# Low-weight ring 32 bytes further along, and the activation buffers placed anew against both weight rings, in a one-core hybrid decoder layer

## The chip, the core and the metric

The kernel is one program on one core of a Trainium2 chip. The metric is device time in microseconds (us) of that core; 1393.51 us is the median of three runs before the change (1393.4 to 1394.25). All arithmetic is in fp32. TensorE multiplies in its fp32r form (a faster, rounded kind of fp32), and each large product is split in a high and a low part so that the result keeps fp32 accuracy.

## What is computed

One layer of a decoder, 256 tokens wide, model width 2048. Cut to what matters:

```
h      = rms_norm(x, norm_mix_g);  proj = h @ w_in                 # 2048 -> 8*512 + 3*2048
o_a, o_b, o_c = hgrn2(...), s5(...), stick_breaking(...)           # three mixers, width 512 each
merged = sum_k sigmoid(gate_k) * (o_k @ w_branch[k]);  x = x + merged @ w_out
up     = causal_depthwise_conv(rms_norm(x, norm_ffn_g) @ w_up, conv_w)   # 2048 -> 2*5632
x      = x + (silu(up[..., :D_FF]) * up[..., D_FF:]) @ w_down            # 5632 -> 2048
```

## The kernel before

Weights stream from HBM in pieces of 8 blocks (a block is 128 x 128, 512 bytes a partition; a piece is 4096 bytes a partition) into a ring of four buffers `raw0` to `raw3`. ScalarE writes the high part of a piece to `w_hi` (L743), VectorE the difference to `w_lo` (L1076); both are rings of four too. Activations are kept transposed, features on the partitions and 256 tokens along the free dimension, with the high part and the low part of a feature tile side by side: `a_raw` and `a_in` (normed input, later the merged branches), `h2` (normed input of the up projection), `act` (hidden activations), and `o_hg`, `o_sb`, `o_s5`, `glu_in` for the branches. One k tile of these takes 2048 bytes a partition, 1024 of them high and 1024 low.

The stages follow one another on TensorE: input projection (tiles 0 to 63, mixers between tiles), GLU, three branches, output projection, up projection, down projection. SP's queue issues the weight loads in that order, each as soon as `w_lo` of the piece four before it is ready. A block is multiplied in one of two ways.

A **pair** (`piece`, L376 and L378), used for input tiles 0 to 7, GLU, output, up and down:

```
pe.matmul(bank[b][:, :], w[:, k * P:(k + 1) * P], a.rearrange("p a t -> p (a t)"), ...)      # w_hi x (high, low): 512 columns
mm = pe.matmul(bank[b][:, 0:SEQ], l[:, k * P:(k + 1) * P], a[:, 0, :], ...)                  # w_lo x high: 256 columns
```

A **triple** (`in_piece` L390, `branch_piece` L416, `plain_piece` L401), used for input tiles 8 to 63, the branches and the last output tile of down: three multiplies of 256 columns, `w_hi` x high, `w_hi` x low, `w_lo` x high. Either way 768 columns pass for one block, and each multiply has a weight load of its own.

TensorE holds one set of weights while the next is being loaded. In the trace a load starts within 0.01 us of the multiply ahead of the one it serves. So while the array streams one operand out of SBUF (the *moving* operand: an activation), the load reads another (the *stationary* operand: a weight block). In a pair, the `w_lo` block is loaded beside the 512-column multiply and the next `w_hi` block beside the 256-column one. In a triple, `w_hi` is loaded beside the first and the third multiply and `w_lo` beside the second.

Buffers have fixed addresses. Each tensor starts where the one before it ends, rounded up to 32 bytes; the names `late`, `early`, `mixing`, `within` and `splits` are scopes that lay several sets over the same space. A tensor called `apart` of 160 bytes a partition, which nothing uses, stands before the scopes:

```
rstd = sb("rstd", [P, SEQ])
var = sb("var", [P, SEQ])
root = sb("root", [P, SEQ])
sb("apart", [P, 40])

late = ExitStack()
act = sb("act", [P, FT, 2, SEQ], F32R, late)
x1 = sb("x1", [P, KT, SEQ], F32, late)
h2 = sb("h2", [P, KT, 2, SEQ], F32R, late)
```

A block is 512 bytes and a k tile 2048, so the distance of an activation buffer from a weight buffer, taken modulo 128, is the same for all blocks of a stage.

Of the kernel before, what the change touches and what calls it, by code (L numbers as in the profile page):

```python
# [38 lines left out]
F32 = mybir.dt.float32  # L39
# [6 lines left out]
P = 128  # L46
# [88 lines left out]
def layer(nc, xT, w_in, w_glu, w_br, w_out, w_up, w_down, norm_mix, norm_ffn, hg_gain, s5_small, s5_b, s5_c,  # L135
          s5_skip, sb_gain, conv, out):
    ctx = ExitStack()
    with ctx:
        def sb(name, shape, dt=F32, scope=None):
            return (scope or ctx).enter_context(nc.sbuf_tensor(name, shape, dt))  # L140


        raw = [sb(f"raw{s}", [P, PIECE * P]) for s in range(RING)]
        w_hi = [sb(f"w_hi{s}", [P, PIECE * P], F32R) for s in range(RING)]
        w_lo = [sb(f"w_lo{s}", [P, PIECE * P], F32R) for s in range(RING)]
        half = [sb(f"half{s}", [P, SEQ]) for s in range(2)]
        ones = sb("ones", [P, P], F32R)
# [18 lines left out]


        late = ExitStack()
        act = sb("act", [P, FT, 2, SEQ], F32R, late)
        x1 = sb("x1", [P, KT, SEQ], F32, late)  # L170
        h2 = sb("h2", [P, KT, 2, SEQ], F32R, late)
        sum_u = sb("sum_u", [P, 2, SEQ], F32, late)
        padded = sb("padded", [P, 2, SEQ + 2], F32, late)
# [3 lines left out]


        early = ExitStack()
        a_in = sb("a_in", [P, KT, 2, SEQ], F32R, early)  # L180
        head = ExitStack()
        x_first = sb("x_first", [P, KT, SEQ], F32, head)
# [1635 lines left out]
```

## Time and profile before

| | |
|---|---|
| median of 3 runs | 1393.51 us (1393.4 to 1394.25) |
| the profiled execution | 1393.05 us |
| its span on the core, first to last instruction | 1391.5 us |
| TensorE matmul busy | 1387.0 us (100%) |
| TensorE weight loads busy (beside matmuls) | 1280.6 us (92%) |
| VectorE busy | 1034.2 us (74%) |
| ScalarE busy | 755.1 us (54%) |
| GpSimd busy | 143.2 us (10%) |
| DMA queue of the weights | 255.89 MB, 57.8% of the 16 engines |

Busy time is the union of instruction records. Matmuls overlap in the pipeline, so a busy TensorE says only that something is in it; how fast it goes is read from the distance between the starts of two multiplies. 1.55 us of the profiled time lies around the span.

### The profile page before, as it was taken

What the parts mean: (1) busy time and instruction counts of PE and PEld (TensorE: products, weight loads), DVE (VectorE), ACT (ScalarE), POOL (GpSimd) and SP (SyncE); (2) the same over time, 40 slices, a digit from 0 to 9 for tenths busy, and PEclk for the clock granted to TensorE, in tenths of its full rate; (3) what the DMA queues carried; (4) which work ended last, traced back from release to release, by engine and by line L of the source; (5) the groups of instructions that cost most, each with busy time, mean ns of one, the idle gap of its engine ahead of it and who ended that gap; (6) DMA issues with size and microseconds to landing.
All of it is one profiled execution on the core that took longest, in us unless ns stands there. A gap on an engine that the chain in (4) does not pass through costs nothing.

```text
span 1391.5 us, 27921 instructions
## 1 busy us (share of the span) xinstructions
PE 1387.0 (100%) x9886; PEld 1280.6 (92%) x9886; DVE 1034.2 (74%) x1427; ACT 755.1 (54%) x1056; POOL 143.2 (10%) x187
## 2 busy tenths in 40 slices
PE   9999999999999999999999999999999999999999
PEld 8999999999999999988888888888888888888888
DVE  7999857899889678776687777777777775455453
ACT  7575676754544554545655555555555554444432
POOL 1200000000000024322111111111111110000000
PEclk9999999999999999999999999999999999999999
DMA  8655545446564656766566555655656656666663
GB/s 287 187 185 180 181 156 179 145 162 198 171 195 161 196 182 218 222 188 193 174 202 193 192 187 182 193 194 185 188 189 194 182 178 198 207 188 201 195 202 111
DMA packets 76513, 261.70 MB, mean 188 GB/s; under 512 B 8800, under 2 KB 10368, under 8 KB 76448
## 3 DMA queue, kind: packets, MB, share of 16 engines
q1 hardware_dynamic: 74304, 255.89, 57.8%
q0 software_dynamic: 1424, 4.37, 1.1%
q8 instruction: 46, 0.75, 0.2%
q10 hardware_dynamic: 720, 0.53, 0.1%
q14 instruction: 19, 0.16, 0.0%
HBM read 258.66 MB, written 2.10 MB: 187 GB/s over the span
## 4 chain that ended last, share of the span: by engine, by line
PE 98%; ACT 1%; DMA 1%; DVE 0%; SPq 0%; issue 0%; ACTq 0%
PE bank L376 40%; PE bank L390 28%; PE bank L378 21%; PE bank L416 5%; PE pair L435 1%; PE bank L401 1%; DMA x_first<-xT 0%; DMA raw<-w_in 0%; PE pair L572 0%; ACT w_hi L743 0%; ACT gates L753 0%; PE pair L441 0%; SPq L298 0%; PE pair L543 0%; ACT L753 0%
## 5 line engine op out<-in xcount | busy, mean ns | idle before, releaser
L1076 DVE TENSOR_TENSOR w_lo<-raw,w_hi 128x1024 fp32r<-128x1024 f32 x496 | 584.8, 1189 | 292.9 <-ACT w_hi L743 288.2
L743 ACT ACTIVATE w_hi<-raw 128x1024 fp32r<-128x1024 f32 x496 | 508.7, 1030 | 411.4 <-PE bank L378 198.5
L376 PE MATMUL bank<-h,w_hi 128*128 128x512 f32 x1408 | 488.4, 390 | 0.0
L378 PE MATMUL bank<-h,w_lo 128*128 128x256 f32 x1408 | 397.1, 282 | 0.0
L390 PE MATMUL bank<-a_in,w_hi 128*128 128x256 f32 x2048 | 362.1, 280 | 0.0
L376 PEld LDWEIGHTS bank<-h,w_hi 128*128 128x128 f32 x1408 | 264.4, 188 | 55.4
L390 PEld LDWEIGHTS bank<-a_in,w_hi 128*128 128x128 f32 x2048 | 311.8, 188 | 3.1 <-issue 2.1
L390 PE MATMUL bank<-a_in,w_lo 128*128 128x256 f32 x1024 | 285.6, 279 | 0.0
L378 PEld LDWEIGHTS bank<-h,w_lo 128*128 128x128 f32 x1408 | 266.1, 189 | 0.0
L376 PE MATMUL bank<-act,w_hi 128*128 128x512 f32 x660 | 228.8, 390 | 0.0
L390 PEld LDWEIGHTS bank<-a_in,w_lo 128*128 128x128 f32 x1024 | 192.5, 188 | 0.0
L378 PE MATMUL bank<-act,w_lo 128*128 128x256 f32 x660 | 186.1, 282 | 0.0
L376 PEld LDWEIGHTS bank<-act,w_hi 128*128 128x128 f32 x660 | 123.9, 188 | 26.0
L378 PEld LDWEIGHTS bank<-act,w_lo 128*128 128x128 f32 x660 | 124.7, 189 | 0.0
L1742 POOL TENSOR_TENSOR padded<-sum_u,rstd 128x256 f32<-128x256 f32 x88 | 73.9, 841 | 413.1 <-DVE sum_u L1097 400.3
L376 PE MATMUL bank<-a_in,w_hi 128*128 128x512 f32 x256 | 88.8, 390 | 0.0
L378 PE MATMUL bank<-a_in,w_lo 128*128 128x256 f32 x256 | 72.2, 282 | 0.0
L1016 ACT ACTIVATE silu<-convd 128x256 f32<-128x256 f32 x43 | 18.0, 418 | 95.9 <-DVE convd L1602 95.9
L1600 DVE SCALAR_TENSOR_TENSOR convd<-padded,taps,convd 128x256 f32<-128x256 f32 x88 | 62.7, 713 | 1.0 <-ACT convd L1036 1.0
L1602 DVE SCALAR_TENSOR_TENSOR convd<-padded,taps,convd 128x256 f32<-128x256 f32 x88 | 54.0, 614 | 11.5
L376 PEld LDWEIGHTS bank<-a_in,w_hi 128*128 128x128 f32 x256 | 48.1, 188 | 10.0
L750 ACT ACTIVATE half<-bank 128x256 f32<-128x256 f32 x135 | 49.4, 366 | 3.7 <-PE bank L378 3.6
(234 smaller groups left out, 1364.4 us busy)
## 6 DMA issues: line engine op xcount, KB each, us to landing
raw<-w_up SPq DMA_DIRECT2D x176, 512.0 KB, 3.7
raw<-w_in SPq DMA_DIRECT2D x156, 512.0 KB, 4.3
raw<-w_down SPq DMA_DIRECT2D x80, 512.0 KB, 4.4
raw<-w_out SPq DMA_DIRECT2D x32, 512.0 KB, 4.2
raw<-w_br SPq DMA_DIRECT2D x16, 512.0 KB, 3.6
raw<-w_br SPq DMA_DIRECT2D x16, 256.0 KB, 3.3
raw<-w_down SPq DMA_DIRECT2D x16, 256.0 KB, 2.7
x_first<-xT SPq DMA_DIRECT2D x8, 256.0 KB, 5.7
```

Of the source, the lines that this page charges most:

```text
L376: pe.matmul(bank[b][:, :], w[:, k * P:(k + 1) * P], a.rearrange("p a t -> p (a t)"), start=first and n == 0, stop=False, skip_group_check= ...
L378: mm = pe.matmul(bank[b][:, 0:SEQ], l[:, k * P:(k + 1) * P], a[:, 0, :], start=False, stop=last and n == len(blocks) - 1, skip_group_check ...
L390: mm = pe.matmul(bank[n % BANKS][:, 0:SEQ], x[:, k * P:(k + 1) * P], src[:, PIECE * h + k, part, :], start=h == 0 and k == 0 and m == 0, s ...
L401: mm = pe.matmul(bank[b][:, 0:SEQ], x[:, k * P:(k + 1) * P], rhs(k, part), start=first and k == 0 and m == 0, stop=last and k == blocks - ...
L416: mm = pe.matmul(bank[b][:, 0:SEQ], x[:, cols], src[:, k, part, :], start=k == 0 and m == 0, stop=k == CT - 1 and m == 2, skip_group_check ...
L743: act_e.activation(w_hi[s][:, 0:blocks * P], raw[s][:, 0:blocks * P], ACT.Copy).then_inc(hi_ready, 1)
L750: act_e.activation(half[j % 2][:, :], bank[j % BANKS][:, SEQ:2 * SEQ], ACT.Copy).then_inc(half_copied, 1)
L1016: act_e.activation(silu[:, :], convd[:, (j - 3) % 4, :], ACT.Silu).then_inc(S("silu_done"), 1)
L1076: ve.tensor_tensor(w_lo[s][:, w], raw[s][:, w], w_hi[s][:, w].bitcast(F32), ALU.subtract).then_inc(lo_ready, 1)
L1600: ve.scalar_tensor_tensor(c, padded[:, j % 2, 1:SEQ + 1], taps[:, t, 1:2], c, ALU.mult, ALU.add).then_inc(S("tap1"), 1)
L1602: ve.scalar_tensor_tensor(c, padded[:, j % 2, 0:SEQ], taps[:, t, 0:1], c, ALU.mult, ALU.add).then_inc(S("conv_done"), 1)
L1742: pool.tensor_tensor(padded[:, j, 2:], sum_u[:, j, :], rstd[:, :], ALU.mult).then_inc(S("up_scaled"), 1)
```

## The change

Four tensors that nothing reads or writes are added; no instruction is added, removed or moved, and every size and shape stays.

```
 raw = [sb(f"raw{s}", [P, PIECE * P]) for s in range(RING)]
 w_hi = [sb(f"w_hi{s}", [P, PIECE * P], F32R) for s in range(RING)]
+sb("apart_weights", [P, 8])
 w_lo = [sb(f"w_lo{s}", [P, PIECE * P], F32R) for s in range(RING)]
...
 late = ExitStack()
+sb("apart_act", [P, 8], F32, late)
 act = sb("act", [P, FT, 2, SEQ], F32R, late)
 x1 = sb("x1", [P, KT, SEQ], F32, late)
+sb("apart_h2", [P, 56], F32, late)
 h2 = sb("h2", [P, KT, 2, SEQ], F32R, late)
...
 early = ExitStack()
+sb("apart_in", [P, 56], F32, early)
 a_in = sb("a_in", [P, KT, 2, SEQ], F32R, early)
```

Start addresses a partition, modulo 128 bytes, as the declared sizes give them. The distances are those of the moving operand past `w_hi` and past `w_lo`, modulo 128 (modulo 256 they are the same numbers):

| buffer | before | after | past `w_hi`, before / after | past `w_lo`, before / after |
|---|---|---|---|---|
| `raw`, `w_hi` | 0 | 0 | | |
| `w_lo` | 0 | 32 | | |
| `a_raw`, `a_in`, `o_*`, `glu_in` | 32 | 32 | 32 / 32 | 32 / 0 |
| `h2` (up) | 32 | 64 | 32 / 64 | 32 / 32 |
| `act` (down) | 32 | 96 | 32 / 96 | 32 / 64 |
| `ones` | 0 | 32 | | |
| `eye`, `lower` | 32 | 64 | | |
| `x1` | 32 | 96 | | |
| `sum_u`, `padded` | 32 | 64 | | |
| `convd`, `silu` | 64 | 96 | | |
| mixers' `proj`, `tmp`, `softp`, `gates` | 32 | 32 | | |

## Rows read from the trace of the kernel before

**Rows 1.** The page's head and busy times of the engines

```profile
span 1391.5 us, 27921 instructions
PE 1387.0 (100%) x9886; PEld 1280.6 (92%) x9886; DVE 1034.2 (74%) x1427; ACT 755.1 (54%) x1056; POOL 143.2 (10%) x187
```

**Rows 2.** The page's chain that ended last, share of the span by line

```profile
PE bank L376 40%; PE bank L390 28%; PE bank L378 21%; PE bank L416 5%; PE pair L435 1%; PE bank L401 1%; DMA x_first<-xT 0%; DMA raw<-w_in 0%; PE pair L572 0%; ACT w_hi L743 0%; ACT gates L753 0%; PE pair L441 0%; SPq L298 0%; PE pair L543 0%; ACT L753 0%
```

**Rows 3.** Waits of TensorE: total us, times, longest us

```profile
PE pair L592 <- POOL ones L1675: 1.2, 1, 1.2
...
PE bank L376 <- DVE w_lo L1488: 0.2, 1, 0.2
```

**Rows 4.** Groups: line, engine, names, shapes, count | busy us, mean ns | idle before

```profile
L376 PE MATMUL bank<-h,w_hi 128*128 128x512 f32 x1408 | 488.4, 390 | 0.0
...
L376 PE MATMUL bank<-act,w_hi 128*128 128x512 f32 x660 | 228.8, 390 | 0.0
...
L376 PE MATMUL bank<-a_in,w_hi 128*128 128x512 f32 x256 | 88.8, 390 | 0.0
...
L376 PE MATMUL bank<-a_raw,w_hi 128*128 128x512 f32 x128 | 45.1, 395 | 0.5 <-DVE w_lo L1076 0.3 <-DVE w_lo L1488 0.2
...
L376 PE MATMUL bank<-glu_in,w_hi 128*128 128x512 f32 x32 | 11.1, 390 | 0.0
```

**Rows 5.** Groups of the triples' third multiply, same columns

```profile
L390 PE MATMUL bank<-a_in,w_lo 128*128 128x256 f32 x1024 | 285.6, 279 | 0.0
...
L390 PE MATMUL bank<-a_raw,w_lo 128*128 128x256 f32 x128 | 35.6, 278 | 0.0
...
L416 PE MATMUL bank<-o_hg,w_lo 128*128 128x256 f32 x64 | 17.8, 279 | 0.0
```

**Rows 6.** Timeline of TensorE, down stage's first pair and first triple: start us, us

```profile
1144.53 0.39 PE L376 MATMUL bank<-act,w_hi 128*128 128x512 f32 x1
...
1373.33 0.40 PE L401 MATMUL bank<-act,w_hi 128*128 128x256 f32 x2
```

**Rows 7.** Timeline, first multiplies of input tiles 9, 11, 54 and 57

```profile
58.15 0.28 PE L390 MATMUL bank<-a_raw,w_hi 128*128 128x256 f32 x1
...
69.45 0.28 PE L390 MATMUL bank<-a_raw,w_hi 128*128 128x256 f32 x1
...
337.51 0.28 PE L390 MATMUL bank<-a_in,w_hi 128*128 128x256 f32 x1
...
354.31 0.28 PE L390 MATMUL bank<-a_in,w_hi 128*128 128x256 f32 x1
```

**Rows 8.** Timeline of TensorE over the two `within` products of the mixers

```profile
262.29 0.39 PE L543 MATMUL pair<-softp_hi,lower 128*128 128x512 f32 x1
...
262.75 0.28 PE L543 MATMUL pair<-softp_hi,lower 128*128 128x256 f32 x1
...
263.23 0.40 PE L543 MATMUL pair<-softp_hi,lower 128*128 128x512 f32 x1
...
263.70 0.28 PE L543 MATMUL pair<-softp_hi,lower 128*128 128x256 f32 x1
...
264.17 0.40 PE L390 MATMUL bank<-a_in,w_hi 128*128 128x256 f32 x2
```

**Rows 9.** Weight loads: one of `within` in the timeline, the up stage's group

```profile
262.52 0.19 PEld L543 LDWEIGHTS pair<-softp_hi,lower 128*128 128x128 f32 x1
...
L378 PEld LDWEIGHTS bank<-h,w_lo 128*128 128x128 f32 x1408 | 266.1, 189 | 0.0
```

**Rows 10.** Groups of the two weight splits, whole kernel

```profile
L1076 DVE TENSOR_TENSOR w_lo<-raw,w_hi 128x1024 fp32r<-128x1024 f32 x496 | 584.8, 1189 | 292.9 <-ACT w_hi L743 288.2
...
L743 ACT ACTIVATE w_hi<-raw 128x1024 fp32r<-128x1024 f32 x496 | 508.7, 1030 | 411.4 <-PE bank L378 198.5
```

**Rows 11.** Busy us by engine in two stretches (input, up), granted clock, DMA

```profile
300.00:400.00 100.00, 100.00 (x900) 98.03 (x899) 90.14 (x115) 50.98 (x60) 0.00 (x0) 1.00 0.54 175
...
700.00:800.00 100.00, 100.00 (x579) 88.67 (x578) 78.21 (x109) 56.73 (x92) 15.55 (x19) 1.00 0.60 196
```

More of the change, by code:

```diff
@@ L144, in layer @@
         w_hi = [sb(f"w_hi{s}", [P, PIECE * P], F32R) for s in range(RING)]
+        sb("apart_weights", [P, 8])
         w_lo = [sb(f"w_lo{s}", [P, PIECE * P], F32R) for s in range(RING)]
@@ L168, in layer @@
         late = ExitStack()
+        sb("apart_act", [P, 8], F32, late)
         act = sb("act", [P, FT, 2, SEQ], F32R, late)
         x1 = sb("x1", [P, KT, SEQ], F32, late)
+        sb("apart_h2", [P, 56], F32, late)
         h2 = sb("h2", [P, KT, 2, SEQ], F32R, late)
@@ L179, in layer @@
         early = ExitStack()
+        sb("apart_in", [P, 56], F32, early)
         a_in = sb("a_in", [P, KT, 2, SEQ], F32R, early)
```

## Prediction, made before the changed kernel ran

> **What bounds the kernel now.** I read the page's busy times first, then the chain, then TensorE's waits, and last the timeline, to see at what pace the multiplies go. TensorE's matmuls are busy for 1387.0 of 1391.5 us [rows 1]. The chain that ended last is TensorE almost alone: the pairs (L376, L378) hold 61%, the triples (L390, L416, L401) 34% [rows 2]. TensorE waits for others next to never: the longest wait is 1.2 us for the first constant, the waits for a weight split are tenths [rows 3]. The clock granted is 1.00, its upper level of 2.4 GHz, in the stretches I looked at [rows 11]. So the time is the number of multiplies times their pace, and only what changes the pace changes the time by much.
>
> The pace: the down stage's pairs begin at 1144.53 us, the triples after them at 1373.33 [rows 6], and 660 pairs lie between [rows 4]: 228.80 / 660 = 346.7 ns for 768 columns. 768 columns at 2.4 GHz take 320.0 ns, so 26.7 ns a pair, 8%, is spent on something else. No wait of TensorE on a semaphore stands in between. Triples show three multiplies in 353.3 ns between input tiles 9 and 11 (32 triples in 11.30 us) and in 350.0 between tiles 54 and 57 (48 triples in 16.80 us) [rows 7]. The instructions are the same there, and so are the addresses modulo 128. The paces 346.7, 350.0 and 353.3 are 3.3 ns apart, which is 8 cycles of 2.4 GHz, the time in which 8 columns (32 bytes) of the moving operand are read. I take this as the sign that the 8% comes from two readers, the moving operand and the weight load beside it, that step on each other in lumps of 3.3 ns, and that the lumps depend on how the two stand to each other. That is an inference, not a row.
>
> **The change, part by part.** No instruction is added or moved, so there is no new wait, no new DMA and nothing to count but the pace. The buffers that nobody reads cost nothing. What moves is the distance of the two readers.
>
> *How much hangs on it.* Up has 1408 pairs and down 660, together 2068; output 256, input 128 and GLU 32, together 416 [rows 4]. Triples with unchanged activations number 1024 + 128 in the input and 3 x 64 in the branches (the other two branches' groups are as the one shown), together 1344 [rows 5].
>
> *Up and down.* In up the load of `w_hi` beside the 256-column multiply goes from 32 to 64 bytes, the load of `w_lo` beside the 512-column one stays at 32. In down both change, to 96 and 64. No operand of this trace stands at 64 or 96, so the cost is bounded from both sides. The low bound is the bare column time, 26.7 ns a pair less: 2068 x 26.7 = 55.1 us less. For the high bound I use the only fp32r products in the trace whose operands stand otherwise, the two `within` products: `lower` and `softp_hi`, `softp_lo` are at the same residue. Their 4 multiplies of 512 and 8 of 256 columns take 264.17 - 262.29 = 1.88 us [rows 8]. At the pace of the big loops they would take 4 pairs and 4 more multiplies of 256 columns, 4 x 346.7 + 4 x 116.7 = 1854 ns, so they are 26 ns slow. Seven of the twelve have a load at the same residue beside them (the others load `ones`, or `w_hi`, 32 away), which is 3.8 ns for each. Part of it may be only the change of shape after the bank loops, since it is one sample of 1.9 us. Two of these a pair in up and down would be 2068 x 7.6 = 15.7 us more. Between those bounds I take one lump of 3.3 ns less for each pair: 2068 x 3.33 = 6.9 us less. The direction comes from the same comparison: 32 apart is faster than 0 apart, so standing further apart may take away another lump. One lump rather than eight, because one lump is what separates any two of the paces that the trace shows.
>
> *Input, branches, GLU, output.* The distance to `w_hi` stays at 32, that to `w_lo` falls from 32 to 0. By the `within` rows each `w_lo` load would then cost 3.8 ns: (416 + 1344) x 3.8 = 6.7 us more. Below, a lump of 3.3 ns a triple is possible, if the spot turns out better: 1344 x 3.3 = 4.5 us less, with 1.4 us from the 416 pairs. The weight loads themselves last the same in both positions, 0.19 us and 189 ns [rows 9], so I take 0 here and keep both ends.
>
> *VectorE, ScalarE and GpSimd* read and write moved buffers too. They have cover: VectorE is busy 78 of 100 us in up and ScalarE 57, and in the input stage VectorE has its tightest stretch, 90 of 100 [rows 11]. The `w_lo` split takes 1189 ns and begins after waits for ScalarE that sum to 288 us, and ScalarE's split in turn waits for TensorE to give buffers back [rows 10]. This costs nothing until VectorE's work in the input grows by a tenth.
>
> *Sum.* 1393.05 us (the profiled execution: span 1391.5 and 1.55 around it) - 6.9 + 0 = 1386.2. The median of the runs lies 0.5 above the profiled execution, so 1386.6 us.
>
> **A rule against it.** The trace shows weight loads busy 92% of the span beside matmuls that are busy all of it, at 346.7 ns a pair against 320.0 of columns [rows 1, 4, 6]. The Trainium skill, page "TensorE: Matmul & The Clock Gate", "Part 2: What happens when you issue a matmul", says that TensorE reads the two operands through two independent ports of SBUF, and that loading the next tile's weights takes no read bandwidth from the multiply that runs. The page "SBUF — State Buffer", "SBUF: two separate sides", says that TensorE's port never waits for anyone. By these two the placement changes nothing and the sum is that of before. The first page's gap between two multiplies (columns at 2.4 GHz and about 2.5 ns) would make a pair 325 ns; the trace has 346.7, so something that the page does not count is there.
>
> **The rivals.**
> *No change, 1393.5 us.* The 26.7 ns are the array's own switching of weights, whatever the addresses. For: the loads last 189 ns at 32 apart and 0.19 us at 0 apart [rows 9], and both paces of the triples occur at one and the same placement. Against: the excess of the `within` products, if it is more than their change of shape. This is also the case in which the change doesn't do what it says.
> *Slower through the low ring, 1400.2 us.* The `w_lo` loads of the input side now start at the residue of the moving operand. Place: L376 and L390, L416. Price: 3.8 ns x 1760 = 6.7 us, with nothing gained in up and down: 1393.5 + 6.7 = 1400.2. It decides as soon as a load at distance 0 costs 1.6 ns or more (2.8 us), if up and down stand still; against a gain of 6.9 in these it needs 5.5 ns or more. If up and down also lose a lump, 1407.
> *Faster by several lumps, about 1373.* Three lumps of 3.3 ns in each pair of up and down: 20.7 us less. For: 26.7 ns are there to be had. Against: nothing in the trace shows such a step. I count it as the far end of my forecast.
> *VectorE becomes late in the input stage.* If moved operands make its operations over 10% longer, the pieces come late. In 390 us of input stage, a further 5% would be 20 us. Nothing speaks for it but that a spot moved; 2 in 100.
>
> **How the numbers follow.** About 0.2%, 2.8 us, is what a measurement of this kernel can tell from no change. My forecast, a gain in up and down with little lost elsewhere, gets 0.43, its own range 1373 to 1390. No change 0.23. Slower through the low ring, with or without up and down, 0.32; VectorE 0.02. Hence faster 0.43, same 0.23, slower 0.34. The range must take in the slower case with one lump more in up and down (1407) in most of its weight and the gain to three lumps; I set it at 1373 to 1405.
>
> **What would show it.** Right: down's 660 pairs take 226.6 us in place of 228.8 (343.3 ns a pair), and up's pairs the same pace; the input tiles stay at 350 or 353 ns a triple; no new waits of TensorE. Wrong by the rule: all paces stay to the tenth of a ns. Wrong by the low ring: triples at 354 ns, output pairs at 350. What would undo the forecast most is that the placement sets which of the two rhythms of the triples appears, since the 1344 triples would then move by 3.3 ns together, 4.5 us either way.

## The result, and the profile after

The changed kernel takes 1403.55 us (median of 4 runs, 1403.22 to 1405.24) against 1393.53: a ratio of 1.0073, with a 95% interval of 1.0061 to 1.0085. It is 10 us slower where 7 us faster was forecast; the stated range, 1373 to 1405 us, held it by 1.5 us, at the end that was put there for slower cases. Two lines of its page:

```profile
span 1401.6 us, 27921 instructions
...
PE 1396.7 (100%) x9886; PEld 1280.9 (91%) x9886; DVE 1034.8 (74%) x1427; ACT 755.2 (54%) x1056; POOL 142.8 (10%) x187
```

The other engines' busy times are those of [rows 1] within 0.6 us; only TensorE's grew, by 9.7. It waits for nobody new, as its waits (total us, times, longest) show against [rows 3]; but the wait for an early `w_lo` in the input is 0.6 us longer:

```profile
PE pair L596 <- POOL ones L1679: 1.2, 1, 1.2
PE bank L380 <- DVE w_lo L1492: 0.8, 1, 0.8
```

The pace itself changed. Rows of TensorE's timeline (start us, us) at the ends of the output, up and down stages (all lines are four further than before; L380 and L382 are the pair, L394, L420 and L405 the triples):

```profile
569.73 0.39 PE L380 MATMUL bank<-a_in,w_hi 128*128 128x512 f32 x1
...
658.47 0.40 PE L380 MATMUL bank<-h,w_hi 128*128 128x512 f32 x1
...
1150.14 0.39 PE L380 MATMUL bank<-act,w_hi 128*128 128x512 f32 x1
...
1383.34 0.28 PE L405 MATMUL bank<-act,w_hi 128*128 128x256 f32 x1
```

Down's 660 pairs take 233.20 us where they took 228.80 [rows 6]: 353.3 ns a pair against 346.7. Output's 256 pairs take 88.74 us, 346.7 ns, as before. Two windows (us, then busy us and instructions of TensorE, its loads, VectorE, ScalarE and GpSimd, granted clock, DMA share, GB/s) answer to [rows 11]:

```profile
300.00:400.00 100.00, 100.00 (x895) 98.03 (x894) 89.67 (x115) 50.96 (x60) 0.00 (x0) 1.00 0.54 175
700.00:800.00 100.00, 100.00 (x575) 87.61 (x574) 78.25 (x110) 56.37 (x92) 15.13 (x18) 1.00 0.61 191
```

In the input 895 multiplies fit in 100 us instead of 900, in up 575 instead of 579; the clock is the same. Stage by stage, from the starts of the first multiplies in both timelines, the 10.2 us of span are: input 2.3, GLU 0.0, branches 0.2, output 0.0, up 3.1, down's pairs 4.4, the rest 0.2. Of the input's 2.3, 0.4 lie ahead of its first triple, where TensorE still waits for its first weights (46.46 us against 46.05). That stretch differs without any change of distances too: e3 below, with all distances as before, has 46.75.

### The profile page after: what moved, and what is told of

It is laid out like the page before. It is cut to its first block, busy times and chain, and to the rows that moved or that the text cites. A ratio compares the mean times of both kernels' runs of the same rounds, so it can differ in the third digit from the quotient of the medians.

```text
span 1401.6 us, 27921 instructions
## 1 busy us (share of the span) xinstructions
PE 1396.7 (100%) x9886; PEld 1280.9 (91%) x9886; DVE 1034.8 (74%) x1427; ACT 755.2 (54%) x1056; POOL 142.8 (10%) x187
## 4 chain that ended last, share of the span: by engine, by line
PE 98%; DMA 1%; SPq 0%; ACT 0%; DVE 0%; issue 0%
PE bank L380 40%; PE bank L394 29%; PE bank L382 21%; PE bank L420 5%; PE pair L439 1%; PE bank L405 1%; DMA x_first<-xT 0%; DMA raw<-w_in 0%; PE pair L576 0%; PE pair L445 0%; SPq L302 0%; PE pair L547 0%; SPq L322 0%; DVE w_lo L1080 0%; ACT w_hi L747 0%; ACT a_raw L913 0%
## 5 line engine op out<-in xcount | busy, mean ns | idle before, releaser
L380 PE MATMUL bank<-h,w_hi 128*128 128x512 f32 x1408 | 491.5, 394 | 0.0
L382 PE MATMUL bank<-h,w_lo 128*128 128x256 f32 x1408 | 393.8, 280 | 0.0
L394 PE MATMUL bank<-a_in,w_hi 128*128 128x256 f32 x2048 | 364.3, 281 | 0.0
L380 PEld LDWEIGHTS bank<-h,w_hi 128*128 128x128 f32 x1408 | 264.6, 188 | 61.0
L394 PEld LDWEIGHTS bank<-a_in,w_hi 128*128 128x128 f32 x2048 | 312.8, 188 | 3.1 <-issue 2.1
L394 PE MATMUL bank<-a_in,w_lo 128*128 128x256 f32 x1024 | 286.5, 280 | 0.0
L382 PEld LDWEIGHTS bank<-h,w_lo 128*128 128x128 f32 x1408 | 264.0, 187 | 0.0
L380 PE MATMUL bank<-act,w_hi 128*128 128x512 f32 x660 | 233.2, 395 | 0.0
L394 PEld LDWEIGHTS bank<-a_in,w_lo 128*128 128x128 f32 x1024 | 192.7, 188 | 0.0
L382 PE MATMUL bank<-act,w_lo 128*128 128x256 f32 x660 | 187.4, 284 | 0.0
L380 PEld LDWEIGHTS bank<-act,w_hi 128*128 128x128 f32 x660 | 124.3, 188 | 28.8
L382 PEld LDWEIGHTS bank<-act,w_lo 128*128 128x128 f32 x660 | 124.3, 188 | 0.0
L380 PE MATMUL bank<-a_in,w_hi 128*128 128x512 f32 x256 | 88.8, 391 | 0.0
L382 PE MATMUL bank<-a_in,w_lo 128*128 128x256 f32 x256 | 71.7, 280 | 0.0
L380 PEld LDWEIGHTS bank<-a_in,w_hi 128*128 128x128 f32 x256 | 47.9, 187 | 10.5
```

The lines of the kernel that those rows point to most:

```text
L394: mm = pe.matmul(bank[n % BANKS][:, 0:SEQ], x[:, k * P:(k + 1) * P], src[:, PIECE * h + k, part, :], start=h == 0 and k == 0 and m == 0, s ...
```

## The experiments

Each kernel is the changed one with other sizes for the four unused tensors, unless the text says more. Written "32/0" is a place 32 bytes past the high ring and 0 past the low one, modulo 128. All paces below are the mean distance between starts in the timeline of the profiled execution, over the stage's pairs or triples, without those that a wait or another product interrupts. Up in the changed kernel is 348.9 ns so; with the one product that stands in its first tile (norm2) the stage's 491.67 us over 1408 pairs are 349.2, the number in the expectations. Where a time has no ratio it is one run.

### Which distance, or whose residue

**e1_low_ring_back**

```
-sb("apart_weights", [P, 8])
 ...
-sb("apart_act", [P, 8], F32, late)      # act: 96 past both rings
+sb("apart_act", [P, 16], F32, late)
 ...
-sb("apart_in", [P, 56], F32, early)     # a_in: 32 past both; h2 64 past both
```

> The low ring goes back to the residue of the high ring; the activations keep their distance past the high ring (input 32, up 64, down 96), so past the low ring they stand 32, 64, 96. Theory D (the pace of a pair is set by the two distances of the moving operand from the weights): input and output pairs as before, 346.7 ns; up and down at paces not seen yet, other than 349.2 and 353.3 if the distance past the low ring counts. Theory A (the moving operand's own residue counts): up 349.2 and down 353.3 ns a pair as in the changed kernel, input as before, about 1401 us. Theory R (the gap between the two weight rings counts): all as before, 1393.5 us.

Measured: 1406.01 us, ratio 1.0086 (1.0069 to 1.0103). Input, output and GLU are as before (output 346.7 ns). Up, at 64/64, goes at 353.3 ns a pair, and down, at 96/96, at 350.0. The timeline's rows at the two ends of down:

```profile
1154.68 0.40 PE L380 MATMUL bank<-act,w_hi 128*128 128x512 f32 x1
...
1385.69 0.28 PE L405 MATMUL bank<-act,w_hi 128*128 128x256 f32 x1
```

231.01 us for 660 pairs is 350.0 ns. The activations kept their own addresses modulo 128 and their distance from the high ring; only the low ring moved, and up became 4.4 ns slower and down 3.3 ns faster than in the changed kernel. Theory A (own residue) and theory R (gap of the rings) both fall.

Who steps on whom can be narrowed down in the changed kernel's own down stage. Other engines and the DMA come and go there, and the pace does not follow them. Three windows of 4, 4 and 6 pairs, from start to start (us, then busy us and instructions of TensorE, its loads, VectorE, ScalarE and GpSimd, clock, DMA share, GB/s):

```profile
1359.67:1361.08 1.41, 1.41 (x10) 1.24 (x9) 0.00 (x0) 0.00 (x0) 0.00 (x0) 1.00 0.76 267
1152.97:1154.38 1.41, 1.41 (x10) 1.24 (x9) 1.37 (x4) 0.78 (x2) 0.85 (x1) 1.00 0.74 279
1158.62:1160.74 2.12, 2.12 (x14) 1.86 (x13) 2.12 (x3) 1.26 (x2) 0.00 (x0) 1.00 0.03 2
```

Each is 353 ns a pair. Over the whole stage, 43 pairs pass while VectorE, ScalarE and GpSimd all stand still, 428 while at least one of them is busy throughout, 90 with a DMA share under 0.05 and 308 with one over 0.80. Every one of these sets has a mean of 353.3 or 353.4 ns, and no pair of the stage lies outside 353 to 354. So the loss in down is no collision with another engine or with a transfer; it lies between TensorE's own reads, loads and multiplies.

**e2_ring_only**

```
-sb("apart_act", [P, 8], F32, late)
+sb("apart_act", [P, 56], F32, late)     # act and h2, like a_in, 32/0
-sb("apart_h2", [P, 56], F32, late)
```

> The low ring stays 32 bytes on, and all activations stand 32 past the high ring and 0 past the low one. Theories D and A: up and down go at the 346.7 ns a pair that the output stage has in the changed kernel, 7.7 us less than that kernel; the input keeps its 2.3 us over before: about 1396. Theory R: up and down stay at 349.2 and 353.3, about 1403.5.

Measured: 1391.28 us, ratio 0.9983 (0.9973 to 0.9992). Faster than either expectation. Output keeps 346.7 ns, but up and down, at the same 32/0, go at 344.4:

```profile
658.86 0.39 PE L380 MATMUL bank<-h,w_hi 128*128 128x512 f32 x1
...
1144.31 0.39 PE L380 MATMUL bank<-act,w_hi 128*128 128x512 f32 x1
...
1371.64 0.28 PE L405 MATMUL bank<-act,w_hi 128*128 128x256 f32 x1
```

(1371.64 - 1144.31) / 660 = 344.4 ns. So the low ring alone gains 4.6 us in the pairs of up and down and loses 2.8 in the input, 0.6 of them ahead of the first triple. And one and the same pair of distances shows two paces, which no theory had. The pace changes inside up: the first tile's pairs still go at 346.7 ns, those behind the norm2 product at 344.4.

**e3_all_shift**

```
+sb("apart_all", [P, 8])
 raw = [sb(f"raw{s}", [P, PIECE * P]) for s in range(RING)]
```
with the other four tensors gone.

> The kernel before with everything from the raw ring on moved 32 bytes: all distances as before, all residues 32 further. Theories D and R: 1393.5 us, every pace as before. Theory A: the moving operand now stands at 64 like up in the changed kernel, 349.2 ns a pair in up, down and output: 2324 pairs by 2.5 ns, 5.8 us slower, about 1399.

Measured: 1393.89 us, ratio 0.9999 (0.9989 to 1.0008). Up and down at 346.7. Where the whole arrangement lies doesn't count; how its parts stand to one another does.

**e4_swap**

```
-sb("apart_act", [P, 8], F32, late)      # act 64/32
-sb("apart_h2", [P, 56], F32, late)
+sb("apart_h2", [P, 8], F32, late)       # h2 96/64
-sb("apart_in", [P, 56], F32, early)     # a_in 64/32
```

> The changed kernel with up and down exchanged (up 96 and 64, down 64 and 32), and input at 64 and 32. Theories D and A: the paces go with the distances: up 353.3 ns (9.3 us over before), down 349.2 (1.6 us over), output 349.2 (0.6 us over), input triples at a pace not seen yet: about 1405 and up. If the paces belong to the stages and not to the distances (theory S): up 349.2, down 353.3, about 1403.5.

Measured: 1409.19 us, ratio 1.011 (1.0094 to 1.0127). Up goes at 353.3 ns and down at 348.9, exactly exchanged:

```profile
1158.64 0.40 PE L380 MATMUL bank<-act,w_hi 128*128 128x512 f32 x1
...
1388.91 0.28 PE L405 MATMUL bank<-act,w_hi 128*128 128x256 f32 x1
```

230.27 / 660 = 348.9. Output and GLU at 64/32 show 348.9 and 348.8 too. The pace goes with the distances and not with the stage.

### Other distances

Kernels of one run each, to see what the pace does along the distances. Their edits are the sizes alone; the expectation of each names the places.

**e5_plus_128**

```
-sb("apart_act", [P, 8], F32, late)
+sb("apart_act", [P, 48], F32, late)
-sb("apart_h2", [P, 56], F32, late)
+sb("apart_h2", [P, 40], F32, late)
```

> Low ring 32 on, input 32 past high and 0 past low, as in the changed kernel; up stands 160 past the high and 128 past the low ring, down 0 and -32. Theory D128 (only distances modulo 128 count): up goes at the 344.4 ns a pair that 32 and 0 gave, 489 - 3 = 485 us for the stage. Theory D256 (modulo 256 or more): up at another pace. Down at 0 past the high ring is new: if the moving operand at the place of the weights is bad, over 350 ns; if nearness is good, under 346.

1403.07 us. Up at 160/128 went at 351.1 ns, neither 344.4 nor 346.7. That speaks for more than modulo 128, but since 32/0 has more than one pace it does not settle it. Down at 0/-32: 346.7, which was neither of the two paces expected there.

**e6_zero_and_128**

```
-sb("apart_weights", [P, 8])
-sb("apart_act", [P, 8], F32, late)
+sb("apart_act", [P, 24], F32, late)
-sb("apart_h2", [P, 56], F32, late)
+sb("apart_h2", [P, 32], F32, late)
```

> Both rings at one residue, up at distance 0 from both, down at 128 from both, input at 0 from both. D128: up and down go at one pace; D256: at two. Theory N (the nearer the better, as 32/0 344.4, 64/32 348.9, 96/64 353.3 suggest): up under 346. Theory C (two readers that start at one place collide): up over 350.

1411.8 us. Output at 0/0 353.3 ns, input triples at 0/0 359.9, up at 0/0 346.8, down at 128/128 351.1. Theory N falls: in output and in the triples zero distance is as slow as any place seen, and up is not under 346. Theory C falls as well, since up is not over 350. Again one placement has two paces: up's first tile goes at 353.3 ns, and the 346.8 begin behind the norm2 product.

**e7_gap_64**

```
-sb("apart_weights", [P, 8])
+sb("apart_weights", [P, 16])
-sb("apart_act", [P, 8], F32, late)
+sb("apart_act", [P, 56], F32, late)
-sb("apart_in", [P, 56], F32, early)
+sb("apart_in", [P, 48], F32, early)
```

> Low ring 64 on. Up stands 32 past high and -32 past low, down 64 past high and 0 past low, input 32 and -32. Theory L (the distance past the low ring sets most, and 0 is best): down about 345, up worse. Theory H (the distance past the high ring sets most, and 32 is best): up about 345, down about 349 or over.

1397.34 us. Up at 32/-32 went at 348.9 ns, but down at 64/0 at 340.0:

```profile
1153.04 0.39 PE L380 MATMUL bank<-act,w_hi 128*128 128x512 f32 x1
...
1377.44 0.28 PE L405 MATMUL bank<-act,w_hi 128*128 128x256 f32 x1
```

224.40 / 660 = 340.0, 6.7 ns less than before. Theory L had the sign of both; theory H is wrong, as 64 past the high ring is here the best place of all.

**e8_gap_96**

```
-sb("apart_weights", [P, 8])
+sb("apart_weights", [P, 24])
-sb("apart_act", [P, 8], F32, late)
+sb("apart_act", [P, 56], F32, late)
-sb("apart_h2", [P, 56], F32, late)
+sb("apart_h2", [P, 48], F32, late)
-sb("apart_in", [P, 56], F32, early)
+sb("apart_in", [P, 32], F32, early)
```

> Low ring 96 on. Up stands 32 past high and -64 past low, down 96 past high and 0 past low, input 0 past high and -96 past low (32 modulo 128). Theory L: down about 345 again, up worse. Theory H: up about 345, down 350 to 353.

1405.76 us. Down at 96/0: 349.3 ns, up at 32/-64: 346.7. So 0 past the low ring is not enough: theory L falls as well. Neither distance alone orders the paces.

**e10_gap_64_in_96**

```
-sb("apart_weights", [P, 8])
+sb("apart_weights", [P, 16])
-sb("apart_act", [P, 8], F32, late)
-sb("apart_h2", [P, 56], F32, late)
+sb("apart_h2", [P, 8], F32, late)
-sb("apart_in", [P, 56], F32, early)
```

> Low ring 64 on, input 96 and 32, up 128 and 64, down 96 and 32 past the two rings. Input and output pairs and down's pairs have the same distances, so by D (with one rhythm) the same pace. Theory H (past the high ring, 32 and 64 are the good places): all of them over 349 ns.

**e11_gap_64_in_0**

```
-sb("apart_weights", [P, 8])
+sb("apart_weights", [P, 16])
-sb("apart_act", [P, 8], F32, late)
+sb("apart_act", [P, 16], F32, late)
-sb("apart_h2", [P, 56], F32, late)
+sb("apart_h2", [P, 8], F32, late)
-sb("apart_in", [P, 56], F32, early)
+sb("apart_in", [P, 40], F32, early)
```

> Low ring 64 on, input 0 and -64, up 192 and 128 (64 and 0 modulo 128), down 160 and 96 (32 and -32 modulo 128). D128: up at 340.0 ns, down at 348.9. D256: up and down at other paces. Input by H over 350 ns a triple.

e10 took 1416.23 us, e11 1407.1. In e10 output and down, both at 96/32, agree at 346.7 ns, which H had over 349; up at 128/64 353.3 (its first tile about 347), input triples at 96/32 360.0. In e11 up at 192/128 350.0, down at 160/96 353.3 and the input triples at 0/-64 353.4. Neither of D128's two numbers appeared. Up's 350.0 is made of distances of 344 and 356 ns in turn.

### One placement, several rhythms

**e9_gap_64_all_64**

```
-sb("apart_weights", [P, 8])
+sb("apart_weights", [P, 16])
-sb("apart_act", [P, 8], F32, late)
+sb("apart_act", [P, 56], F32, late)     # act, h2, a_in all 64/0
-sb("apart_h2", [P, 56], F32, late)
```

> Low ring 64 on, every activation 64 past the high and 0 past the low ring, which gave 340.0 ns a pair in down. Theory D (the distances set the pace): up, down, output and GLU all at 340.0, 2356 pairs by 6.7 ns, 15.7 us less than before; triples at a pace not seen yet, 353.3 if like 64 and 32, which adds 4.5 us: 1378 to 1382. Theory S (340 belongs to the down stage): up stays at 346 to 349.

Measured: 1402.15 us, ratio 1.0061 (1.0044 to 1.0078). Output goes at 340.0 ns, up and down at 350.0, all at 64/0. Theory D alone fails here. The timeline shows where it turns: up's first tile still runs at 340 ns, then comes the norm2 product (L439, an fp32 product in the middle of the pairs; the trace has two records, x2, for one fp32 multiply), and behind it 350.

```profile
571.12 0.39 PE L380 MATMUL bank<-a_in,w_hi 128*128 128x512 f32 x1
...
658.16 0.39 PE L380 MATMUL bank<-h,w_hi 128*128 128x512 f32 x1
...
662.92 0.39 PE L380 MATMUL bank<-h,w_hi 128*128 128x512 f32 x1
663.15 0.28 PE L382 MATMUL bank<-h,w_lo 128*128 128x256 f32 x1
663.26 0.39 PE L380 MATMUL bank<-h,w_hi 128*128 128x512 f32 x1
663.49 0.28 PE L382 MATMUL bank<-h,w_lo 128*128 128x256 f32 x1
663.61 0.59 PE L439 MATMUL pair<-root,ones 128*128 128x256 f32 x2
663.85 0.58 PE L380 MATMUL bank<-h,w_hi 128*128 128x512 f32 x1
...
1151.24 0.40 PE L380 MATMUL bank<-act,w_hi 128*128 128x512 f32 x1
...
1382.24 0.28 PE L405 MATMUL bank<-act,w_hi 128*128 128x256 f32 x1
```

87.04 us for output's 256 pairs is 340.0 ns; 231.00 for down's 660 is 350.0.

**e12_kick_before_out** is e2 with this ahead of the output stage:

```
+start_product("norm2")
+for _ in range(2):
+    pe.matmul(product("norm2")[:, 0:P], ones[:, :].bitcast(F32), ones[:, :].bitcast(F32), start=True, stop=True, skip_group_check=True)
```

> The kernel with the low ring 32 on and everything 32 past the high ring, with two more 128-column fp32 multiplies on constants before the output stage (their result is overwritten later). Addresses stay. Theory P (one placement has several rhythms, and how a stage is entered picks one): the output pairs leave 346.7 ns and may go at the 344.4 that up has at the same distances. Rival: 346.7 belongs to the output stage, and stays.

1396.34 us. Output's 256 pairs now go at 344.8 ns on average (88.28 us between the two rows below, entry included), and up and down, 344.4 in e2, at 346.7 with nothing changed in them. Theory P has its sign: the two paces of 32/0 changed places. As in e2 the second change comes at the norm2 product, now from 344.4 in up's first tile to 346.7 behind it.

```profile
570.98 0.48 PE L380 MATMUL bank<-a_in,w_hi 128*128 128x512 f32 x1
...
659.26 0.39 PE L380 MATMUL bank<-h,w_hi 128*128 128x512 f32 x1
```

**e13_kicks_64_0** and **e14_kicks_changed** asked whether the changed kernel's own paces are only such an entry. Both have extra multiplies of five kinds, whose result is never read, at eight places in up and down (e13 with tensors of 16, 56, 0 and 16 columns in the order of the diff):

```
+kick(['', 'a', 'c', 'b'][j], h2)        # up's first four tiles: none, fp32 128 columns, fp32r 256, fp32 64
+kick("d", h2)                           # before up's loop: fp32r 512
+kick("e", act)                          # before down: fp32r 128
+kick(['a', 'c', 'd', ''][j], act)       # down's last four tiles
```

> The changed kernel with the same extra multiplies. If the distances 64 and 32, 96 and 64 have one rhythm each, up stays at 348.9 and down at 353.3 ns a pair behind every one of them, and the loss of the change belongs to the distances. If some stretches go at 346.7 or less, the loss is partly a matter of how the stages are entered.

1404.49 us. Up's pairs average 349.0 ns and down's 353.5, entries included (the extra multiplies' own time is not), and no tile of either stands out. At 64/32 and 96/64 no second rhythm came out, in this kernel, the changed one or e4.

> Low ring 64 on, up and down 64 and 0 past the rings, input 160 and 96. One to three extra multiplies on constants or on activations (their result is never read) stand before up's tiles 1 (fp32, 128 columns), 2 (fp32r, 256) and 3 (fp32, 64), before up's loop (fp32r, 512), before down (fp32r, 128) and before down's last three pair tiles (fp32 128, fp32r 256, fp32r 512). Theory P (several rhythms, the entry picks): the pairs behind some of them go at 340.0 ns, behind others at 350.0. Theory D alone: one pace throughout. The input triples at 160 and 96 show 346.7 ns, as the last tile of down did at these distances.

1387.86 us. Up's pairs average 340.2 ns and down's 340.3, entries included; behind every extra multiply the pace is 340.0, and no stretch at 350 appeared. Theory P had said that one would, so here it missed; the first extra multiply stands right behind the norm2 product, as in e15 below. The input at 160/96 missed too: 355.1 ns a triple in place of 346.7, and 353.3 a pair in output, though the branches at the same place had 346.7.

**e15_all_64_one_kick** is e9 with one multiply behind the norm2 product, **e16_before_one_kick** the placement of before with the same one:

```
 fp32_product("norm2", [((0, P, 0, SEQ), ones[:, :].bitcast(F32), root[:, :], True, True)])
+wait_taken(pe, PRODUCTS[-2])
+pe.matmul(pair[(M["norm2"] + 1) % 2][:, 0:P], ones[:, :].bitcast(F32), ones[:, :].bitcast(F32), start=True, stop=True, skip_group_check=True)
```

> Low ring 64 on, all activations 64 and 0 past the rings, and one fp32 multiply of 128 columns on constants right behind the norm2 product in up's first tile. Theory P (the norm2 product threw the pairs from the rhythm of 340.0 ns into that of 350.0, and another entry brings them back): up and down at 340.0, so 2068 pairs by 10 ns, 20.6 us less than without the multiply: 1381.5. Rival: without the other extra multiplies up and down stay at 350.0, about 1402.

> The placement of before with the same extra multiply. The pairs at 32 and 32 have shown one pace, 346.7 ns, in every stage and kernel so far: the same time as before within 0.3 us. If another rhythm exists there too, up and down show it: 350 would give 1400, 343 would give 1387.

e15: 1381.42 us, ratio 0.9911 (0.9897 to 0.9925). e16: 1394.14 us, ratio 1.0002 (0.9992 to 1.0011), all pairs at 346.7. In e15's timeline the extra multiply (L679) stands behind norm2, and the pairs behind it are back at 340:

```profile
663.10 0.59 PE L439 MATMUL pair<-root,ones 128*128 128x256 f32 x2
663.53 0.38 PE L679 MATMUL pair<-ones 128*128 128x128 f32 x2
663.67 0.48 PE L380 MATMUL bank<-h,w_hi 128*128 128x512 f32 x1
...
1137.05 0.39 PE L380 MATMUL bank<-act,w_hi 128*128 128x512 f32 x1
...
1361.45 0.28 PE L405 MATMUL bank<-act,w_hi 128*128 128x256 f32 x1
```

(1361.45 - 1137.05) / 660 = 340.0 ns. Against e9 one multiply of 128 columns, with the wait instruction ahead of it, is worth 20.7 us; by themselves the two are worth nothing at the placement of before. This version beats both kernels, by 12.6 us and 22.1 us. It keeps a loss in the input and the branches, whose triples take 353.4 ns at 64/0 against 350.0 and 350.4 before.

The pairs' paces together, for the places between 0 and 96 past the high ring that decide something:

| past high / past low | pace, ns a pair | where |
|---|---|---|
| 64/0 | 340.0; 350.0 | e7, e13, e15, output of e9; up and down of e9 |
| 32/0 | 344.4; 346.7 | up, down of e2, output of e12; output of e2 and changed, up, down of e12 |
| 32/32 | 346.7 | before, e3, e16, all stages; output of e1 |
| 96/32 | 346.7 | e10, output and down |
| 32/-32 | 348.9 | e7, output and up |
| 64/32 | 348.9 | changed, e4 (three stages), e14 |
| 96/0 | 349.3 | e8 |
| 96/96 | 350.0 | e1 |
| 96/64 | 353.3 | changed, e4, e14 |
| 64/64 | 353.3 | e1 |
| 0/0 | 346.8; 353.3 | e6, up; e6, output |
| 0/-32, 0/-64, 32/-64 | 346.7 | e5, down; e11, output; e8, up |
| 0/-96 | 346.9; 351.7 | e8, input; e8, output |

## Why the prediction was wrong

**What bounds the kernel** was right: TensorE's pace, no new wait, no new transfer, and the clock at its upper level throughout. Of the 10.2 us of span at most 0.6 lie in a wait, for an early `w_lo`. The rival of a late VectorE did not come: 89.67 of 100 us busy in the input stretch against 90.14.

**That the pace depends on the distances** was right, and what the rule against it says of this change, that all paces stay, is refuted here. The sections "Part 2: What happens when you issue a matmul" (page "TensorE: Matmul & The Clock Gate") and "SBUF: two separate sides" (page "SBUF — State Buffer") of the Trainium skill have the two reads of TensorE independent of each other and of everyone. Between kernels with the same instructions the pairs go from 340.0 to 353.3 ns as buffers move by 32 bytes, and not at all when everything moves together (e3). That rests on the timed kernels e1 to e4, e9 and e15, and the windows shown under e1 rule out the other engines and the DMA for down. That it is the two reads that step on each other, and where in the memory or the array, was not shown.

**The step that failed** is the term for up and down, "one lump of 3.3 ns less for each pair", 6.9 us. It was got by running a line through two points: 0 apart slower than 32 apart, hence 64 and 96 apart faster still. In its place the runs showed 2.2 ns more a pair at 64/32 and 6.7 ns more at 96/64: 3.1 us and 4.4 us, 7.5 of the 10.2. The first point came from the `within` products, 26 ns slow with `lower` 0 apart, and that reading does not hold. In e7 and e13, where by the declared sizes none of these multiplies has a weight load at its own residue beside it (`lower` 64 away, `ones` 96, `w_hi` 32), the same twelve take 1.88 us as before; e13's rows:

```profile
264.90 0.40 PE L547 MATMUL pair<-softp_hi,lower 128*128 128x512 f32 x1
...
266.78 0.40 PE L394 MATMUL bank<-a_in,w_hi 128*128 128x256 f32 x2
```

In e1 and e3, at 0 apart like before, they take 1.86. So those 26 ns were no price of standing 0 apart. For the pairs 0/0 is 6.7 ns slower than 32/32 in output but not in up (e6), and from there on the pace does not go on falling: 32/32 346.7, 64/64 353.3, 96/96 350.0. A pair has two loads with a distance each, and one moves against the other; neither alone orders the table. Nothing of that could be read from the trace of before, where all large products stand at 32/32. Nor is 3.3 ns a unit in which all paces differ: 344.4 and 348.9 each lie 2.2 ns from 346.7 (and the 32 triples in 11.30 us, from which the prediction read 353.3, are 353.1). The bounds, 55 us less and 15.7 us more, held it.

**The second term, input, branches, GLU and output at 0,** was mis-sized by 2.5 us: input 2.3 and branches 0.2. 0.4 of that is waiting ahead of the first triple. The rival "slower through the low ring" named this place and 6.7 us. Its price per load, 3.8 ns, came from the same `within` products and was wrong for pairs: output at 32/0 is at 346.7 as before, and up and down at 32/0 even gain 2.2 ns (e2). For most triples it is the right sign and too large: the branches 351.1 against 350.0 ns, the input's `a_in` tiles 352.4 against 350.4. The 128 triples of `a_raw` went the other way, 351.1 against 352.2. So the low ring 32 further is by itself a gain of 2.5 us of 1393.8 (e2), and what made the kernel slower is where up's and down's activations were put. The rival had nothing happen in up and down; its time, 1400.2, was nearest by chance.

**The worry at the end,** that a placement has more than one rhythm, was right in kind and understated: it holds for pairs as well, up to 10 ns each (e9, e15), where the whole spread of the table is 13. For up and down of the change, the step that failed, it did not matter. The paces 348.9 and 353.3 held through the exchange of stages and eight extra multiplies (e4, e14).

**Left open:** whether the distances count modulo 128 or 256 (e5's up at 160/128 had 351.1 ns, which the place 128 nearer did not show; and 160/96 had 353.3 in the input's and output's pairs of e13 and in e11's down, where 32/-32 had 348.9 to 349.0 in the input, output and up of e7. That speaks for more than 128, though a further rhythm is not ruled out), why the input's triples at 160/96 go at 355.1 and the branches' at 346.7, what makes a product between pairs change the rhythm, and what the readers step on.

## What to carry to other kernels

When TensorE is busy all of the time with a weight load beside every multiply, read its pace from the starts of the multiplies: what stands above the columns' time (here 8%) may hang on how the moving buffer stands to the weight buffers, 32 bytes at a time, and the best place is found by trying, since no line through two points finds it. One kernel tries several at once, if each stage has its own place, and the pace by stage tells them apart. Then look at whether the pace is one rhythm from the first multiply to the last: something small in between may have thrown it, and something small may bring it back.

## What was unexpected of the hardware

Pairs of one and the same placement and instructions ran for hundreds of microseconds at 340.0 or at 350.0 ns, at 344.4 or at 346.7, according to what went before them on TensorE. An fp32 product of 256 columns threw the pairs from 340 to 350 (64/0, e9), from 346.7 to 344.4 or the other way (32/0, e2 and e12) and from 353.3 to 346.7 (0/0, e6), and left them as they were at 32/32 and 64/32. At 64/0 one more fp32 multiply of 128 columns behind it put them back, and in five timed runs of e15 the time stayed within 1380.79 to 1382.07. Triples too had two paces at one placement, 346.7 ns in the branches and 355.1 in the input, both at 160/96 (e13); what picks between them was not tested.
